# A hybrid decoder's attention steps: the product with v for two heads at once, alternating by key block, ahead of the transposes

## What is computed

```python
def attend(q, kg, vg, valid):
    logits = jnp.einsum('bqhd,bqkhd->bqhk', q, kg) * HEAD_DIM ** -0.5
    logits = jnp.where(valid[:, :, None, :], logits, -jnp.inf)
    p = jax.nn.softmax(logits, axis=-1)
    return jnp.einsum('bqhk,bqkhd->bqhd', p, vg)
```

## Time and profile before

| what | value |
|---|---|
| median of three runs | 1636.9 us (1636.0 to 1640.32) |
| the profiled execution's own time | 1633.77 us |
| its span | 1632.2 us |
| PE matmul busy | 1497.3 us, 92% of the span |
| PE weight loads busy | 1370.3 us, 84% |
| DVE, ACT, POOL busy | 784.8, 574.7, 209.2 us |
| granted TensorE clock, mean | 0.94 |
| attention steps, layer one and two | about 185 to 305 us and 990 to 1107 us |

### The profile page before, as it was taken

The page is one execution under the profiler, slowest core; times in us unless marked ns, Lnnn a source line. Parts: engine busy times, 40 slices in busy tenths (PEclk is TensorE's granted clock), DMA queues, the critical chain, the costliest instruction groups (busy, mean ns, idle before and its releaser), DMA issues. The chain is left out here.

```text
span 1632.2 us, 28778 instructions
## 1 busy us (share of the span) xinstructions
PE 1497.3 (92%) x11550; PEld 1370.3 (84%) x11550; DVE 784.8 (48%) x1747; ACT 574.7 (35%) x907; POOL 209.2 (13%) x140
## 2 busy tenths in 40 slices
PE   4999989987999999999769998899869999999996
PEld 4899876675999999999658987757849999999994
DVE  5499864734433333222346987657263333322224
ACT  4442232533433433222244422335343333322222
POOL 1333211210000000000040432112100000000000
PEclk7999998997999999999869999999979999999997
DMA  6443205112233332233055322051203333322321
GB/s 238 112 126 90 78 9 152 39 58 63 65 90 90 90 90 84 67 91 90 17 198 134 101 78 72 1 152 56 78 27 91 90 90 91 94 78 72 89 78 53
DMA packets 222686, 141.19 MB, mean 87 GB/s; under 512 B 13482, under 2 KB 218642, under 8 KB 222070
## 3 DMA queue, kind: packets, MB, share of 16 engines
q1 hardware_dynamic: 220006, 132.55, 27.8%
q0 software_dynamic: 2592, 7.48, 1.5%
HBM read 124.64 MB, written 11.77 MB: 84 GB/s over the span
## 5 line engine op out<-in xcount | busy, mean ns | idle before, releaser
L1755 DVE TENSOR_TENSOR w_lo<-ring,w_hi 128x1024 fp32r<-128x1024 f32 (+2 forms) x164 | 179.7, 1096 | 444.0 <-ACT w_hi L1159 444.0
L596 PE MATMUL PS<-u_hi,w_hi 128*128 128x260 f32 x1664 | 341.4, 287 | 22.7 <-DVE y_lo L1835 13.1
L1159 ACT CAST w_hi<-ring 128x1024 fp32r<-128x1024 f32 (+2 forms) x168 | 159.2, 948 | 556.0 <-PE PS L596 556.0
L596 PE MATMUL PS<-u_hi,w_lo 128*128 128x260 f32 x1664 | 337.6, 284 | 0.0
L596 PE MATMUL PS<-u_lo,w_hi 128*128 128x260 f32 x1408 | 284.6, 283 | 0.0
L596 PEld LDWEIGHTS PS<-u_hi,w_hi 128*128 128x128 f32 x1664 | 260.1, 191 | 26.6 <-DVE y_lo L1835 13.9
L596 PEld LDWEIGHTS PS<-u_hi,w_lo 128*128 128x128 f32 x1664 | 258.8, 190 | 0.0
L596 PEld LDWEIGHTS PS<-u_lo,w_hi 128*128 128x128 f32 x1408 | 217.9, 189 | 0.0
L596 PE MATMUL PS<-hid_hi,w_hi 128*128 128x260 f32 x704 | 144.4, 287 | 5.7 <-DVE hid_lo L1879 5.7
L596 PE MATMUL PS<-hid_hi,w_lo 128*128 128x260 f32 x704 | 143.5, 285 | 0.0
L596 PE MATMUL PS<-hid_lo,w_hi 128*128 128x260 f32 x704 | 142.9, 285 | 0.0
(11 more groups left out here) (326 smaller groups left out, 2247.1 us busy)
## 6 DMA issues: line engine op xcount, KB each, us to landing
ring<-in_ffn_gate SPq DMA_DIRECT2D x44, 512.0 KB, 3.8
ring<-in_ffn_up SPq DMA_DIRECT2D x44, 512.0 KB, 3.8
ring<-in_w_in SPq DMA_DIRECT2D x36, 512.0 KB, 3.8
ring<-in_ffn_down SPq DMA_DIRECT2D x32, 384.0 KB, 3.4
ring<-in_ffn_down SPq DMA_DIRECT2D x32, 320.0 KB, 3.1
ring<-in_w_out SPq DMA_DIRECT2D x16, 512.0 KB, 5.8
x_store<-x SPq DMA_DIRECT2D x2, 2080.0 KB, 15.2
x<-x_store SPq DMA_DIRECT2D x2, 2080.0 KB, 8.2
```

The source lines that it names most:

```text
L596: ins = pe.matmul(to[:, h, :], w[:, k - base, :], a[k][:, h * HALF:(h + 1) * HALF], start=(begin and w is whi and a is a_hi), stop=(end an ...
L1159: act.copy(w_hi[part % 2][:, 0:n, :], raw[part % 4][:, 0:n, :]).then_inc(part_hi, 1)
L1755: dve.tensor_tensor(w_lo[part % 2][:, 0:n, :], raw[part % 4][:, 0:n, :], w_hi[part % 2][:, 0:n, :].bitcast(F32), ALU.subtract).then_inc(pa ...
```

## The change

Only PE's program changes. The product with v of head-steps `j - 3` and `j - 2` (an even and an odd head of the same query block) is issued in step `j` for odd `j` from 3 on, ahead of the transposes, and the two heads alternate inside the loop over key blocks. Even steps issue no product with v. The operands, their number and the place of the results are the same, and each head still counts up `mixed` at its last product.

```diff
                         if STATES_FROM <= j < STATES_FROM + NS // 2:
                             spread_states(j - STATES_FROM)
+                        if j >= 3 and j % 2:
+                            blk, h = STEPS[j - 3]
+                            pe.wait_ge(prob_t_ready, j - 1)
+                            if h == 0 and blk >= 1:
+                                pe.wait_ge(mixed_out, blk)
+                            at = (blk % 2) * W + (h // 2) * P
+                            for kb in range(blk + 1):
+                                for i in (j - 3, j - 2):
+                                    r = HD * (i % 2)
+                                    last = pe.matmul(bank(7)[r:r + HD, at:at + P], tok_v[:, kb, (i % HEADS) * HD:(i % HEADS + 1) * HD],
+                                                     prob_t[:, i % 2, kb * P:(kb + 1) * P], start=(kb == 0), stop=(kb == blk))
+                                    if kb == blk:
+                                        last.then_inc(mixed, 1)
                         if 1 <= j <= len(STEPS):
...
                         if 0 <= j < DENSE_STEPS:
                             feature_products(PER_STEP[1])
-                        if j >= 2:
-                            i = j - 2
-                            blk, h = STEPS[i]
-                            r = HD * (h % 2)
-                            pe.wait_ge(prob_t_ready, i + 1)
-                            if h == 0 and blk >= 1:
-                                pe.wait_ge(mixed_out, blk)
-                            at = (blk % 2) * W + (h // 2) * P
-                            for kb in range(blk + 1):
-                                last = pe.matmul(bank(7)[r:r + HD, at:at + P], tok_v[:, kb, h * HD:(h + 1) * HD],
-                                                 prob_t[:, i % 2, kb * P:(kb + 1) * P], start=(kb == 0), stop=(kb == blk))
-                            last.then_inc(mixed, 1)
```

## The result

The changed kernel takes 1627.67 us in the median of 6 runs (1626.32 to 1630.18). The kernel before, run beside it, takes 1636.45 (6 runs, 1634.76 to 1640.32). The ratio is 0.9945, with a 95% interval of 0.9931 to 0.996: 8.8 us faster. The forecast was 1628.2.

A forecast was written before the change was run, and what follows sets the result against it. PE was taken as the bound, busy 1497.3 of 1632.2 us. Savings of 4.34 us per layer, 8.7 in all, took the profiled 1633.77 to 1625.1; 3.1 up to the median gave 1628.2, range 1623.5 to 1633.5.

The forecast's parts named there:

- Full overlap: Products with v: two alternating heads cost what one costs, 1.09 us for 16 records, as the state products at L932 do.
- The first rival: Products with v: a pair's heads run one after the other, 8.7 - 8.8, about 1637.0 us; chance 0.08.
- The exit into the transposes: From a pair's block into the transposes: 0.20 us, already in the block price; possible ends 0.11 and 0.48.
- The saving ahead of the long wait is absorbed: Heads 0 and 1: step 2's saving is lost in PE's 3.24 us wait at 200.77, where DVE sets the time.
- The new wait for DVE: Step 14, second to third L770: PE's way falls to 5.09 us against DVE's 5.45, a new wait of 0.36.
- The second rival: Steps 13 to 17: DVE's state chain binds, 2.48 us per layer are lost, 1633.2 us; chance 0.10.
- Transposes late: Odd steps: transposes behind the pair come later, PE waits 12.2 us and no saving shows, 1649.1 us; chance 0.04.
- The sum: Attention steps: removed blocks and fewer changes of form on PE save 4.34 us per layer, 8.7 in all.
- The term for heads 2 and 3: Second pair of heads, early steps: 2 x 0.45 - (0.18 + 0.45) = 0.27 us saved per layer.
- The step stretches 4.4 us shorter per layer: Sign expected in the profile after: each layer's attention steps are 4.4 us shorter.
- the term for the clock: Attention steps: new positions shift some stretches at 1.2 GHz either way; 3 us allowed, none forecast.
- The long weight stages follow PE and shift whole: Behind the steps: PE's end of the steps anchors the next stages, so the whole saving reaches the end.

The follow-up runs named there:

- e1: Changed kernel with both heads of a pair written to the same PSUM partitions, one head after the other; 1639.62 us, ratio 1.0014 to the kernel before.
- e8: Changed kernel with the odd heads' products with v left out; 1629.11 us, ratio 0.9957 to the kernel before.
- e6: Changed kernel with pairs only up to step 9 and the old order from step 10 on; 1638.16 us, ratio 1.0017 to the kernel before.
- e7: Changed kernel with pairs only from step 11 on and the old order for head-steps 0 to 7; 1636.27 us, ratio 1.0002 to the kernel before.
- e10: Kernel before with two extra 512-column products ahead of layer one as a delay; 1636.95 us, ratio 1.0009 to the kernel before.
- e12: Same as e6, with two extra 512-column products ahead of layer one as a delay; 1639.30 us, ratio 1.0017 to the kernel before.
- e4: Changed kernel with the pair moved to the start of the odd step, ahead of the logits; 1635.40 us, ratio 0.9998 to the kernel before.
- e11: Same as e4, with two extra 512-column products ahead of layer one as a delay; 1636.70 us, ratio 1.0014 to the kernel before.

## Why the prediction was right, and where it was not

The number was right, 1628.2 for 1627.67, and so was the side. The savings on PE were argued rightly. That they came out as time to within 0.5 us is partly luck, by the last two points below. The steps of the argument, one by one:

- *Full overlap* was right: 1.09 us for 16 records as for 8, by the changed kernel, e1 and e8. L932 was the right row to read. The first rival, no overlap, would have given 1637.0; e1, which has no overlap, measured 1639.62.
- *The exit into the transposes*, taken as 0.20 between 0.11 and 0.48, was right: blocks of 4, 8 and 16 records cost 0.37, 0.59 and 1.02 to the transpose, as one head's cost into other forms.
- *The saving ahead of the long wait is absorbed*: right. The first wait of L682 took up what PE was early, 3.24 us became 3.62 in the first layer, and the wait behind the cast is 1.69 as it was. The timeline of PE after:

```profile
202.75 0.80 PE L682 MATMUL PS<-u_hi,w_hi 128*128 128x260 f32 x2 [3.62 <-ACT hid L1103]
...
214.48 0.51 PE L682 MATMUL PS<-u_hi,w_hi 128*128 128x260 f32 x2 [1.69 <-ACT hid L1103]
```

- *The new wait for DVE* was right: 0.30 us in place of 0.36, between the same two L770. The second rival, the later steps bound by DVE, fell with it: in the first layer this is PE's only wait for DVE's chain.
- *Transposes late* (the slower rival) fell: ACT and DVE waited 6.7 and 2.7 us longer in all, and PE 0.4.
- *The sum* was nearly right at full speed, and a little low: in steps 7 to 17 it is 3.9 to 4.0 us per layer for 3.58, with 0.8 for 0.30 in the early part (e6) and 3.5 to 3.8 for 3.28 in the late one (e7). The term for heads 2 and 3 leaves out the 0.05 for the transposes that the pairs of block 1 pay, without a reason; that is 0.1 us in all.
- *"The step stretches 4.4 us shorter per layer" was wrong.* They are 0.7 and 0.8 us shorter in the first pair of traces and 1.1 and 1.3 in the second. The step that failed is the term for the clock: "I allow 3 us and forecast none". Steps 7 to 17 have 6.8 us more at 1.2 GHz per layer, and with PE busy nearly throughout that cost 3.4 us per layer, 6.8 in all, more than twice what was allowed. I took the clock of the earlier trace rows as if it belonged to the stretch. It belongs to one trace: with a delay ahead, the kernel before has the changed kernel's 17.1 us itself (e10).
- *"The long weight stages follow PE and shift whole" was wrong as well*, to the other side: they became 1.5 to 2.5 us per layer shorter, in and around the stretches at 1.2 GHz. The two misses largely cancel, 6.8 us lost in the steps and 4.0 to 4.9 won behind them in the two pairs of traces, and that the forecast gave neither and still came so near is luck. That the two can be linked is borne out by e10, where the old order has 3.2 us more in the steps and 3.3 less behind them in the first layer (2.6 in the second). It isn't a law: in e6 and e12 the second layer got nothing back.

By the sum of steps and the part behind, three traces against three, 6.8 us of the change is accounted for, of 8.7 forecast and 7.7 to 8.8 measured in medians.

**What stays open.** I did not find what puts the clock down at 280.0 us. PE had worked without a pause on L817 (64 rows) and L770 (8 rows), and the same two stand in the same order in the kernel before. The Trainium skill (TensorE: Matmul & The Clock Gate, Part 1, "HAM oscillation — how this bites in real kernels") ties such falls to PE's idle gaps. Here the fall at 280 comes with PE busy 42.70 of the 43 us from 262 on, and the missing 0.30 lies at 291.92, behind it. So idle gaps do not explain this one. The other stretch that the changed kernel has more than before, 3.4 us from 239.1 us on, comes 2.5 us behind a wait of 1.69 us for ACT; the kernel before has the same wait and no such stretch. One other form wasn't tried: the pair at the end of the odd step, where the old block stood. By the waits in the code, ACT's copy of that step's transposes would then wait for the pair; what that costs was not measured. No kernel of the twelve beats the changed one.

## What to carry to other kernels

Float32 products of 64 output rows that go to different halves of PSUM's partitions should alternate product by product: the second of two equal ones was free here, and with one head's products issued after the other's only a small part was hidden. Where a stage mixes wide and narrow products, price an edit at full speed and then keep some us for the clock, in both directions. Measure the finished edit, not its parts: here each half of a change alone was no gain or a loss, and an order that was 1 to 2 us per layer better at full speed (e4) ended nearly 8 us behind. And where a change is as small as this one, compare traces over the stretch and what follows it together: here the clock took 6.8 us in the one and gave part of it back in the other.

## What was new about the hardware

- Alternating halves hide the second product's weight load as well as its multiplication: 16 records hold PE for 1.02 us, 0.064 each, against 0.118 (1.89 / 16) in one half, though each has a weight load of 0.137 us in the median. With one head's products after the other's it is 1.51.
- The granted clock falls to 1.2 GHz also while PE is busy throughout (279.90 to 283.30: clock 0.52, PE 3.40 of 3.40). In the same 11 steps, with almost the same work, the time at 1.2 GHz summed up to anything from 10.2 to 41.0 us.
- The pattern can be steady for a kernel: 17.1 us in each layer of three traces of the changed kernel. Yet two more products far ahead changed it in the kernel before from 10.2 to 17.1, and the whole took only 1.4 us longer. Other kernels had it different from layer to layer (e1, e4, e7, e11).
